# A hybrid attention and mixture-of-experts step: the sample tile of the input projection in four column groups of the array, and a later request for the first expert's up weights

## The reference, cut to what matters

```python
z = _rms(x, norm1_g) @ w_in                 # 1024 -> 2584 columns: q, keys and values, gates, retention, memory queries
...                                         # attention (compressed, selected, window), retention, memory attention
x = x + mix @ w_out
h = _rms(x, norm2_g)
logits = h @ w_router + b_router            # 32 experts, the 4 best of each token
up = h[rows of e] @ w_up[e] + b_up[e]       # 1024 -> 2048
act = min(up[:, :1024], 7) * sigmoid(1.702 * min(up[:, :1024], 7)) * (clip(up[:, 1024:], -7, 7) + 1)
y = act @ w_down[e] + b_down[e]             # 1024 -> 1024, weighted by the gate and summed per token
```

## Time and profile before

| | us |
|---|---|
| median of 3 runs | 2806.73 (2805.57 to 2809.25) |
| profiled execution, device time | 2808.08 |
| its span in the trace | 2806.4 |
| PE busy | 2596.8 (93%) |
| DVE, ACT, POOL busy | 935.5, 642.7, 489.5 |
| bytes moved | 533.63 MB, 190 GB/s over the span |

### The profile page before, as it was taken

One profiled execution on the slowest core, in us unless ns is written; L12 is line 12 of the kernel. 1 busy time (PEld: TensorE's weight loads), 2 busy tenths in 40 slices (PEclk: granted clock), 3 DMA queues, 4 the chain that ended last, 5 costly groups with the idle time before them and its releaser, 6 DMA issues.

```text
span 2806.4 us, 44495 instructions
## 1 busy us (share of the span) xinstructions
PE 2596.8 (93%) x18096; PEld 2126.2 (76%) x18096; DVE 935.5 (33%) x2614; ACT 642.7 (23%) x1619; POOL 489.5 (17%) x476
## 2 busy tenths in 40 slices
PE   7999995998998869939999999999999999999994
PEld 3555544545666644519999999999999999999994
DVE  1122132216756533542422222323232322322221
ACT  1111111115756522210111111111111111111111
POOL 0000002201000010220232231323232322212211
PEclk9999996998999979969999999999999999999997
DMA  5000018305000153227687788888999999999995
GB/s 196 12 23 21 14 48 172 61 1 178 1 1 1 61 148 109 78 91 292 229 272 267 261 278 279 279 297 289 309 302 329 314 315 322 315 327 322 303 332 158
DMA packets 281953, 533.63 MB, mean 190 GB/s; under 512 B 52482, under 2 KB 93410, under 8 KB 281538
## 3 DMA queue, kind: packets, MB, share of 16 engines
q1 hardware_dynamic: 233122, 472.68, 47.6%
q0 software_dynamic: 33504, 46.98, 7.9%
q10 hardware_dynamic: 15120, 11.08, 1.4%
HBM read 492.21 MB, written 42.96 MB: 191 GB/s over the span
## 4 chain that ended last, share of the span: by engine, by line
PE 54%; DMA 1%; POOL 0%; DVE 0%; issue 0%; SPq 0%; POOLq 0%; ACT 0%; DVEq 0%; ACTq 0%
PE up L2167 36%; PE down L2178 18%; DMA w_up<-summed_rows 1%; DMA slot_rows<-slot_tokens_gates 0%; POOL x_rows L2125 0%; SPq L2115 0%; DMA summed_rows<-y_rows,row_index_cur 0%; POOL summed_rows L2131 0%; DMA x_rows<-h_rows,row_index_cur 0%; PE down L2184 0%; POOLq L2011 0%; ACT y_rows L2197 0%; DVEq L2076 0%; DVE glu L2276 0%; DVE w_down L2362 0%
## 5 line engine op out<-in xcount | busy, mean ns | idle before, releaser
L2167 PE MATMUL up<-hT,w_up 128*128 128x128 f32 (+19 forms) x8192 | 1007.9, 286 | 12.0 <-DVE hT L2256 12.0
L2167 PEld LDWEIGHTS up<-hT,w_up 128*128 128x128 f32 x8192 | 1004.8, 191 | 12.3 <-issue 12.3
L2178 PE MATMUL down<-actT,w_down 128*128 128x128 f32 (+19 forms) x4096 | 508.1, 286 | 0.5 <-DVE actT L2281 0.4
L2178 PEld LDWEIGHTS down<-actT,w_down 128*128 128x128 f32 x4096 | 503.6, 191 | 1.9 <-DVE actT L2281 0.9
L2131 POOL DMA_INDIRECT summed_rows<-y_rows,row_index_cur x153 | 240.9, 1575 | 1085.8 <-ACT y_rows L2197 1049.2
L2276 DVE TENSOR_SCALAR glu<-up,b_up_cur 128x128 f32<-128x128 f32 (+19 forms) x256 | 93.6, 366 | 1005.7 <-PE up L2167 987.3
L311 PE MATMUL zp<-w_in,xnT 128*128 128x512 f32 (+3 forms) x896 | 353.7, 550 | 1.4 <-DVE xnT L481 1.4
L311 PEld LDWEIGHTS zp<-w_in,xnT 128*128 128x128 f32 (+1 forms) x896 | 152.4, 186 | 177.5 <-issue 173.7
L2208 ACT ACTIVATE sig<-glu 128x128 f32<-128x128 f32 (+19 forms) x256 | 82.9, 324 | 862.0 <-DVE glu L2276 762.1
L2216 ACT ACTIVATE yT<-down,b_down_cur 128x128 f32<-128x128 f32 (+19 forms) x256 | 97.6, 381 | 394.0 <-PE down L2178 394.0
L2125 POOL DMA_INDIRECT x_rows<-h_rows,row_index_cur x153 | 149.5, 977 | 59.6 <-issue 46.0
(11 more groups left out here) (404 smaller groups left out, 1901.9 us busy)
## 6 DMA issues: line engine op xcount, KB each, us to landing
w_up<-in_w_up SPq DMA_DIRECT2D x128, 2048.0 KB, 10.8
w_down<-in_w_down SPq DMA_DIRECT2D x64, 2048.0 KB, 8.6
w_in<-in_w_in SPq DMA_DIRECT2D x5, 2048.0 KB, 12.7
x<-in_x_prompt SPq DMA_DIRECT2D x8, 512.0 KB, 3.8
window_rows<-in_x_prompt SPq DMA_DIRECT2D x8, 512.0 KB, 3.8
summed_rows<-cache_rows SPq DMA_DIRECT2D x8, 512.0 KB, 2.7
h_rows<-h SPq DMA_DIRECT2D x8, 512.0 KB, 3.6
w_up<-summed_rows SPq DMA_DIRECT2D x8, 512.0 KB, 8.2
```

What stands on the lines that cost most here:

```text
L2167: mm = nc.tensor.matmul(up[c % 2][:, h, :N], U[c // 4][:, h, kk, w0:w0 + P], hT[:, kk, :N], start=(kk == 0), stop=(kk == KC - 1))
L2178: mm = nc.tensor.matmul(dn[d % 2][:, :N], Dn[:, kk // 4, kk % 4, d * P:d * P + P], aT[:, kk, :N], start=(kk == 0), stop=(kk == KC - 1))
```

## The change

It has two parts. In the sample tile the 2584 columns are no longer taken slice after slice. `project_sample` puts four slices of 512 columns side by side: the matmul of slice n writes partitions 32n to 32n+31 of `zp[0]`, so the four use four different column groups of the array; the order is contraction step outside, slice inside, 32 matmuls in a row and one semaphore increment at their end. The remaining 536 columns are cut into four pieces of 134 and go the same way into `zp[1]`. Between and behind the two groups stands the same other work in the same order. ACT copies four times 32x512 after the first group and four times 32x134 after the second.

The second part takes the request for the first up weights out of `phase_out` and puts it at the head of SP's program in `phase_experts`, behind a wait for the slot list (`s_il`, both of its transfers).

```diff
@@ phase_project, tensor
+            def project_sample():
+                t = PT
+                pe.wait_ge(s_xnT, 2 * t + 2)
+                pe.wait_ge(s_zev, zs(t) - 1)
+                for c in range(KC):
+                    for n in range(4):
+                        mm = nc.tensor.matmul(zp[0][32 * n:32 * n + 32, :], xnT[t % 2][:, c, :SR], w[:, c, 512 * n:512 * n + 512],
+                                              start=(c == 0), stop=(c == KC - 1))
+                mm.then_inc(s_zmm, 4)
+                pre(t + 1)
+                post(t - 1, 2)
+                pe.wait_ge(s_zev, zs(t))
+                for c in range(KC):
+                    for n in range(4):
+                        c0 = 2048 + REST * n
+                        mm = nc.tensor.matmul(zp[1][32 * n:32 * n + 32, :REST], xnT[t % 2][:, c, :SR], w[:, c, c0:c0 + REST],
+                                              start=(c == 0), stop=(c == KC - 1))
+                mm.then_inc(s_zmm, 2)
+                for step in (3, 4, 5):
+                    post(t - 1, step)
@@ phase_project, scalar
+            def evict_sample():
+                ...
+                act.wait_ge(s_zmm, zs(t) + 4)
+                ...
+                for n in range(4):
+                    nc.scalar.copy(zz[:SR, 512 * n:512 * n + 512], zp[0][32 * n:32 * n + 32, :]).then_inc(s_zev, 1)
+                    if n == 0:
+                        pre(t + 1)
+                evict_post(t - 1, 2)
+                act.wait_ge(s_zmm, zs(t) + 6)
+                for n in range(4):
+                    c0 = 2048 + REST * n
+                    ins = nc.scalar.copy(zz[:SR, c0:c0 + REST], zp[1][32 * n:32 * n + 32, :REST])
+                ins.then_inc(s_zev, 2)
+                evict_post(t - 1, 3)
@@ phase_out, sync
             sp.wait_ge(s_n, 1)
-            first = sp.value_load(k.order[0:1, 0:1], min_val=0, max_val=NE - 1)
-            wu = i["w_up"][0].rearrange("e (k p) (h q n) -> e p k h q n", p=P, h=2, q=2)
-            for g in range(2):
-                sp.dma_start(k.early[:, g], wu[bass.ds(first, 1), :, :, g, 0, :].rearrange("o p k n -> (o p) k n")).then_inc(s_u, 16)
@@ phase_experts, sync
+            first = ordered_expert(sp, 0)
+            sp.wait_ge(s_il, 32)
+            for g in range(2):
+                sp.dma_start(k.early[:, g], wu[bass.ds(first, 1), :, :, g, 0, :].rearrange("o p k n -> (o p) k n")).then_inc(k.s_u0, 16)
```

More of the change, by code:

```diff
@@ L152, in phase_project @@
     NA = NT + MT
+    REST = (IN - 2048) // 4
     SL = [(n * 512, min(512, IN - n * 512)) for n in range(6)]
@@ L378, in _ @@
             for t in range(NA):
-                project(t)
+                if t == PT:
+                    project_sample()
+                else:
+                    project(t)
             post(NA - 1, 2)
@@ L411, in evict_z @@
                             evict_post(t - 1, step)
+            def evict_sample():
+                t, zz = PT, z[PT % 2]
+                act.wait_ge(s_zmm, zs(t) + 4)
+                act.wait_ge(s_out[t % 2], stored(t - 2))
+                act.wait_ge(s_pool, t - 1)
+                act.wait_ge(s_o, t - 1)
+                for n in range(4):
[9 more added lines that the diff above has]
+                evict_post(t - 1, 3)
             def squares(t):
@@ L456, in _ @@
                     squares(t - 1)
-                evict_z(t)
+                if t == PT:
+                    evict_sample()
+                else:
+                    evict_z(t)
             squares(NA - 1)
```

## The result

The changed kernel takes 2785.16 us (median of 4 runs, 2783.38 to 2788.24) against 2807.99 for the kernel before, run beside it (4 runs, 2805.57 to 2813.01). The ratio is 0.9915, with a 95% interval of 0.9903 to 0.9927: 22.8 us or 0.85% faster, where 22.9 us (2783.8) were forecast. The profiled execution took 2788.24 us, with a span of 2786.5, 19.8 us less than the profiled execution of before. In what follows "the tile" is the stretch from the sample tile's first matmul to the memory tile's first (42.43 us before, by the earlier trace rows), and "the start" is the stretch from the barrier ahead of the experts to their first matmul (1241.87 to 1263.80 before, 21.93 us).

A forecast was written before the change was run, and what follows sets the result against it. PE was taken as the bound in the experts and the sample tile. Sample tile -20.5 and later weight request -2.4 gave -22.9 us: 2785.2 profiled, 2783.8 median; own range 2779 to 2787, 8 in 10 within 2778.5 to 2789.5.

The forecast's parts named there:

- First group, 7.05 us: Sample tile: 64 records in 16 rounds of four take 7.05 us, as long as one slice did before.
- the rival of streams that slow each other: Sample tile: four long streams side by side give three times instead of four, 2.4 us more, 2786.2 us; chance 6%.
- the one in which a change of group empties the array: Sample tile's two groups: each record costs its whole duration, 55 us against 35.1, total 2829.0 us; chance 2%.
- Wait for `xs`, 3.1 us: Sample tile, after the first group: PE waits 3.1 us for ACT's and DVE's chain, formerly hidden by three slices.
- The clock, 1.0 us: Sample tile: the new wait may bring a half-clock stretch; 1.0 us lost, bounds nothing to 3.4 us.
- the rival of 6 us: Sample tile: PE stays at half clock from 364.7 into the memory tile, 6 us more, 2788.8 us; chance 7%.
- Wait for `rT`, 1.0 us: Sample tile, after `post(7, 3)`: PE waits 1.0 us for ACT's `rT` copies, which follow four small copies taking 0.8.
- The weights of the memory tiles stay covered: Sample tile: weights asked for at 361.6 land at 370.1, covered by 5.4 us before the memory tile.
- The issue taken out of `phase_out`, 0: End of `phase_out`: removing SP's 1.05 us of issue gains 0, between 0 and -1.1 us.
- Slot list 2.7, last gather 4.2: Start of the experts: list lands in 2.7 us instead of 6.54, last gather in 4.2 instead of 2.70.
- The rival of a list that costs 6.5 us by itself: Listed first; experts' start: weights don't hold up the list, PE starts 2.7 us later, total 2788.9 us; chance 14%.
- Part 2 together, -2.4: Experts' start: PE begins at 1261.4 instead of 1263.80, -2.4 us, bounds -4.6 and +3.0.

The follow-up runs named there:

- experiment 4: Changed kernel with the loops of both groups turned, slice outside and contraction step inside: 2808.49 us, ratio 0.9999 to the kernel before.
- experiment 5: Changed kernel with the transposes that wait for `xs` moved on PE behind the second group: 2781.05 us, ratio 0.9906 to the kernel before.
- experiment 6: Changed kernel with PE's `xs` transposes behind second group and `post(7, 3)`, ACT's copies of `z` last: 2775.44 us, ratio 0.9884 to the kernel before.
- experiment 2: Changed kernel with the up weights' request left in `phase_out`, so only the sample tile changed: 2790.84 us, ratio 0.9938 to the kernel before.
- experiment 3: Kernel before with only the later request for the up weights, sample tile slice by slice: 2805.53 us, ratio 0.9991 to the kernel before.
- experiment 12: The kernel before once more, unedited, for a third profile of the old sample tile: 2805.73 us, ratio 0.9994 to the kernel before.

## Why the prediction was right, step by step

The forecast of 22.9 us met the measured 22.8. Its mechanism held in each part; four sizes were off, by up to 0.9 us each. That the two numbers agree to 0.1 us is luck: by start times the two changed stretches gave 21.5 us and not 22.9 (at the end of this section).

- **The experts keep a gain whole.** Right: 1504.64 of 1505.00 us busy.
- **First group, 7.05 us.** Right, 7.07. The rows, with two rounds of 512 columns or eight of 256, did tell what sixteen rounds of 512 would do. Of the Trainium skill's factors ("TensorE: Matmul & The Clock Gate", "Part 3: Packing small matmuls — row/col tiling"), 3.07 for four row tiles and 2.38 for three column tiles, neither fits four column tiles: here it is 27.5 / 7.07 = 3.9. So the rival of streams that slow each other is refuted, and with it the one in which a change of group empties the array; experiment 4 shows the opposite, that only a change of group lets the next matmul in beside the one under way.
- **Wait for `xs`, 3.1 us.** Right, 3.15, and by that chain: experiments 5 and 6 move the transposes behind the second group and the wait goes.
- **The clock, 1.0 us.** Mis-sized. Behind the wait, `xTp` and `post(7, 2)` take 3.25 us from start to start instead of 2.19, the second group 2.22 instead of 1.9, the output 2.82 instead of 2.5: 1.7 us. In experiment 6 the same instructions without the waits run at 1.00, and there the output takes 1.99 and not 2.5: the forecast's 2.5 was itself read from rows in which the clock was 0.86 on the mean (392 to 397 before). The forecast's upper bound was 3.4; the rival of 6 us was not met in any of the six profiles of this tile (22.9 to 23.3 us). That such a wait brings the lower clock each time is not shown: in experiment 4 the transposes behind a wait of 3.13 us take 1.09 us, and the clock stays at 1.00 up to 395.
- **Wait for `rT`, 1.0 us.** Mis-sized, 1.29: the four copies took 1.08 us and not 0.8.
- **Scores to output, 2.26.** Right, 377.99 - 375.73 = 2.26.
- **The weights of the memory tiles stay covered.** Right: issued at 365.00, landed at 373.4, 7.4 us ahead of the memory tile (5.4 foreseen). In experiment 6, where that tile starts 7 us earlier, the cover is gone and 0.42 us of waiting are there.
- **Part 1 together, -20.5.** Measured in the profile 22.95 against 42.43: -19.5. Against the third profile of the old tile (42.70) it is -19.8.
- **The issue taken out of `phase_out`, 0.** Right. In both profiles POOL comes last to that barrier: its first instruction behind it has stood idle 4.3 us on POOL's own sequencer, behind the indirect transfer issued at 1236.62, while SP's issue had ended at 1240.29. From that transfer's issue to the start of the next phase it is 5.25 us before and in experiment 2, with SP's issue, and 5.26 in the changed kernel, without it.
- **Slot list 2.7, last gather 4.2.** Both mis-sized, 2.12 and 5.11; 6.9 foreseen for the sum, 7.23 measured. The rule of the Trainium skill ("DMA: Bandwidth & Descriptors", "Anatomy of one DMA"), by which the estimate for the list was 2.1 us, is fitted there to transfers that GpSimd issues; the 2.12 of this list, which ACT issues, agrees with it. The rival of a list that costs 6.5 us by itself is refuted. The gather beside the weights was put halfway between its two rows, and lies near the upper of them (5.7).
- **Part 2 together, -2.4.** In the profile -2.0, in experiment 3 about 2.5 us of time. Two waits end close to each other, as foreseen, `hT` last, by 0.9 us.

The terms that the profiles show sum to -21.5, 1.3 less than the medians differ; the spread of the half-clock stretches in unchanged code (below) is larger than that.

Two of the foreseen signs did not come: the memory tile starts at 380.81 and not near 375.5, and PE's first up matmul comes 19.0 us earlier (1244.80) and not 24. The whole span closes as follows: the tile starts 3.3 us later, takes 19.5 less, from the memory tile to the barrier it is 0.8 less (844.07 for 844.89), the start 2.0 less and the experts 0.9 less, together 19.9. The 3.3 us are no part of the change (experiment 12).

Some numbers of the forecast do not follow from its own sum. The start in the first rival is 1266.2 + 0.55 = 1266.8, so 2789.1 and not 2788.9, and "about 24 us earlier" should have been 22.9. The upper end of its own range, 2787, has the upper bound of the clock in it but not the +3.0 of a late start, which only the first rival carries. None of them changes the outcome.

## What to carry to other kernels

A matmul that fills a quarter of the array's columns costs as much as a full one (16 records of 512 columns in 7.05 us here, 7.11 for full ones in experiment 6); four of them in different column groups cost one, if they alternate in PE's instruction row. Once a stretch has shrunk, list every chain that it covered and ask in which order the engines behind it do their work: here a third more of the tile's gain (by the traces 5 to 6.6 us on 19.5) lay in putting a handful of ACT's copies, for which nobody waited, behind those for which PE did, in the order of PE's steps that this allowed, and in the clock that came with it. For a small transfer on the critical path look at what was issued shortly before it: a lead of 3.4 us for 4 MB cost it 4.4 us; but bytes put off behind it meet the next transfer, and of the 4.4 only 2.0 remained.

## What the runs showed that was not expected

**Where the half-clock stretches fall differs from run to run, in the same code.** Around 100 us, in the projection of tile 1, PE is busy all the time in every profile. The granted clock (the number before the last two) of before:

```profile
97.00:104.00 7.00, 7.00 (x26) 3.38 (x25) 5.81 (x17) 0.68 (x3) 0.17 (x2) 1.00 0.00 1
```

of the changed kernel:

```profile
97.00:104.00 7.00, 7.00 (x24) 4.16 (x25) 3.85 (x11) 1.08 (x5) 0.57 (x3) 0.62 0.00 0
```

and of the kernel before in experiment 12:

```profile
97.00:104.00 7.00, 7.00 (x23) 4.21 (x24) 3.86 (x11) 1.24 (x5) 0.75 (x4) 0.55 0.00 0
```

Where the sample tile starts (354.4 to 360.7 us in the fourteen profiles with identical work ahead of it) is set by such stretches. From PE's first matmul of the projection at 17 us to the tile, the time at clock 0.50 is 13.2 us before, 20.4 in the changed kernel and 26.1 in experiment 5 (with the first 3 to 5 us, in which the records stand 0.85 us apart), and the tile starts at 354.55, 357.86 and 360.66; with half of that time taken off, the way from the first matmul is 330.9, 330.7 and 330.6 us. Between the memory tile and the barrier, too, the profiles spread, from 839.2 to 844.9 us. So a single profile can't be used to tell a gain of 3 us by its span. The same short stretch of code, from start to start, tells more: the changed kernel's tile takes 22.9 to 23.3 us in its six profiles (with and without part 2), though 16.3 to 17.7 with the copies last. What decides where the stretches fall was not tried.

**Four records pair up at a change of column group even when the slices follow one another** (experiment 4): 22.59 us instead of 27.5. How many matmuls ahead PE may start was not measured otherwise.
